# Second-half low parts of each weight tile on GpSimd instead of VectorE, in a hybrid attention encoder step

## The reference, cut to what matters

```
z = einsum('bld,dc->blc', h, w_in)          # one input projection
fq, fk, fv, fg, ff, sq, sk, sv, sg = split(z)
fo = fox_attention(fq, fk, fv, lf) * silu(fg)      # 16 heads, forget gates, causal
so = swa_attention(sq, sk, sv, sinks, rel_bias) * silu(sg)   # 16 heads, 4 kv heads, window 128
out = einsum('blc,cd->bld', concatenate([fo, so]), w_out)
y = layer_norm(ALPHA * h + out, ln_g, ln_b)
```

## Time and profile before

| | |
|---|---|
| median of 3 runs | 1078.89 us (1078.78 to 1079.07) |
| the profiled execution | 1078.65 us, span of the trace 1077.1 us |
| PE busy | 1053.2 us (98%) |
| DVE busy | 609.4 us (57%) |
| ACT busy | 436.6 us (41%) |
| POOL busy | 50.4 us (5%) |
| low halves on DVE (L796) | 132, mean 1222 ns, 160.3 us |

### The profile page before, as it was taken

The page is one execution under the profiler, slowest core; times in us unless marked ns, Lnnn a source line. Parts: engine busy times, 40 slices in busy tenths (PEclk is TensorE's granted clock), DMA queues, the critical chain, the costliest instruction groups (busy, mean ns, idle before and its releaser), DMA issues.

```text
span 1077.1 us, 20572 instructions
## 1 busy us (share of the span) xinstructions
PE 1053.2 (98%) x7617; PEld 983.4 (91%) x7617; DVE 609.4 (57%) x1493; ACT 436.6 (41%) x1078; POOL 50.4 (5%) x99
## 2 busy tenths in 40 slices
PE   7999999999999999999999999999999999999996
PEld 7999999999999999999999999999999878888885
DVE  6655465554546455364654676554776674333486
ACT  6444344443444344443444454344544553211310
POOL 1010000000000000000010000000000000000000
PEclk9999999999999999999999999999999999999998
DMA  9142223222222312313612212122122144222423
GB/s 334 54 137 90 75 98 108 92 72 100 89 71 100 108 56 85 108 63 110 200 68 92 87 46 78 52 91 96 48 78 77 56 170 163 78 78 83 185 65 117
DMA packets 20810, 106.65 MB, mean 99 GB/s; under 512 B 3216, under 2 KB 3632, under 8 KB 11488
## 3 DMA queue, kind: packets, MB, share of 16 engines
q1 hardware_dynamic: 14960, 83.13, 21.6%
q0 software_dynamic: 5808, 22.95, 6.5%
HBM read 95.18 MB, written 14.17 MB: 102 GB/s over the span
## 4 chain that ended last, share of the span: by engine, by line
PE 91%; DVE 4%; issue 3%; ACT 1%; DMA 0%; DVEq 0%; ACTq 0%; SPq 0%
PE ps L1142 58%; PE ps L1289 18%; PE ps L1259 5%; PE ps L1237 4%; PE ps L1221 2%; PE ps L1220 2%; DVE small L888 1%; DVE tb L874 1%; PE ps L1172 1%; PE ps L1273 1%; ACT wh L619 0%; DMA x_raw<-in_xT 0%; DVE tb L905 0%; DVE small L901 0%; DVE wl L796 0%
## 5 line engine op out<-in xcount | busy, mean ns | idle before, releaser
L1142 PE MATMUL ps<-xh,wh 128*128 128x288 f32 (+1 forms) x1664 | 506.6, 304 | 0.0
L1142 PE MATMUL ps<-xl,wh 128*128 128x288 f32 (+1 forms) x1664 | 493.6, 297 | 0.0
L1142 PE MATMUL ps<-xh,wl 128*128 128x288 f32 (+1 forms) x1664 | 493.2, 296 | 0.0
L1142 PEld LDWEIGHTS ps<-xh,wh 128*128 128x128 f32 x1664 | 313.9, 189 | 8.7 <-issue 7.2
L1142 PEld LDWEIGHTS ps<-xl,wh 128*128 128x128 f32 x1664 | 314.1, 189 | 0.0
L1142 PEld LDWEIGHTS ps<-xh,wl 128*128 128x128 f32 x1664 | 313.5, 188 | 0.0
L796 DVE TENSOR_TENSOR wl<-w_raw,wh 128x1024 fp32r<-128x1024 f32 x132 | 160.3, 1222 | 76.5 <-ACT wh L619 74.0
L1289 PE MATMUL ps<-wh,mix_parts 128*128 128x512 f32 x576 | 185.4, 391 | 0.0
L665 ACT ACTIVATE tb<-tb,small 128x256 f32<-128x256 f32 (+5 forms) x160 | 82.6, 516 | 214.8 <-DVE small L884 135.2
L619 ACT ACTIVATE wh<-w_raw 128x1024 fp32r<-128x1024 f32 x132 | 137.9, 1053 | 77.1 <-PE ps L1289 70.5
L1289 PEld LDWEIGHTS ps<-wh,mix_parts 128*128 128x128 f32 x576 | 108.2, 188 | 22.5 <-DVE mix_parts L1012 0.3
(11 more groups left out here) (112 smaller groups left out, 854.4 us busy)
## 6 DMA issues: line engine op xcount, KB each, us to landing
w_raw<-in_w_all SPq DMA_DIRECT2D x66, 1024.0 KB, 4.8
cbc<-c_rows POOLq DMA_DIRECT2D x16, 360.0 KB, 4.1
x_raw<-in_xT SPq DMA_DIRECT2D x7, 592.0 KB, 9.7
rows<-in_x_p POOLq DMA_DIRECT2D x4, 1024.0 KB, 5.3
out_y_p<-rows SPq DMA_DIRECT2D x16, 256.0 KB, 2.5
rel_copies<-rel_rows POOLq DMA_DIRECT2D x1, 3072.0 KB, 15.8
out_fvT<-vT POOLq DMA_DIRECT2D x8, 296.0 KB, 2.4
out_fkT<-kT POOLq DMA_DIRECT2D x8, 296.0 KB, 2.4
```

The lines of the kernel that those rows point to most:

```text
L1142: ins = nc.tensor.matmul(ps[:, st.bank(k, h), 0:width], a[k % 2][:, w], b[:, ko, first:first + width], start=(ko == 0 and i == 0), stop=(k ...
```

## The change

In every stretch but the opening and the final one, half 1 of each weight tile's low part is computed by POOL (a new `weights_low` there) and no longer by DVE. `w_low` becomes two semaphores, one per half, with every wait counted anew. POOL's program no longer runs each stretch as one short list: it now follows the steps as the others do, with its DMA issues put at the steps `scores_done`, `values_done` and `STEPS + 1`, and `weights_low` at step 5 of each tile. The `rel_copies` DMA and the wait for it stay ahead of the stretch's steps. 48 of the 132 halves move (28 in the Fox loop, 20 behind it).

```diff
@@ -475,23 +475,24 @@
                                      (sink[:], sinks.partition_broadcast(P))):
                         sp.dma_start(dst, src).then_inc(small_loaded, 16)
 
-            def load_weights(n, slot, halves):
-
-                sp.wait_ge(w_high, halves)
-                sp.wait_ge(w_low, halves)
+            def load_weights(n, slot, split):
+
+                for half in range(2):
+                    sp.wait_ge(w_low[half], split)
                 sp.dma_start(w_raw[slot][:], w_all[bass.ds(n, 1)].rearrange("a p n -> p (a n)")
                              ).then_inc(w_loaded[slot], 16)
 
 
-            load_weights(2, 0, 3)
+            load_weights(2, 0, 1)
             with sp.Fori(1, W_TILES // 2 - 1) as j:
-                load_weights(2 * j + 1, 1, 4 * j)
-                load_weights(2 * j + 2, 0, 4 * j + 2)
-            load_weights(W_TILES - 1, 1, 2 * W_TILES - 4)
+                load_weights(2 * j + 1, 1, 2 * j)
+                load_weights(2 * j + 2, 0, 2 * j + 1)
+            load_weights(W_TILES - 1, 1, W_TILES - 2)
 
             for i, (dst, src) in enumerate(((gain, ln_g), (shift, ln_b))):
                 sp.wait_ge(w_high, 2 * (W_TILES - 1 + i))
-                sp.wait_ge(w_low, 2 * (W_TILES - 1 + i))
+                for half in range(2):
+                    sp.wait_ge(w_low[half], W_TILES - 1 + i)
                 sp.dma_start(dst[:], src.partition_broadcast(P)).then_inc(norm_loaded, 16)
             for i, m in enumerate(last_order):
                 for j in range(NORM_CUTS):
@@ -550,48 +551,64 @@
                                    .broadcast_to([N_HEADS, P, REL])).then_inc(bias_copied, 16)
                     pool.wait_ge(bias_copied, 16)
                 if kv is not None:
-
-                    for h in range(2):
-                        pool.wait_ge(evacuated[h], st.n0 + 1)
                     row = (kv if st.own is Fox else kv - FOX_PAIRS) * P
-                    out = fvT if st.own is Fox else svT
-                    pool.sem_inc(pool_passed, 1)
-                    pool.dma_start(out[bass.ds(row, P), :], vT[:]).then_inc(v_stored, 16)
-                if st.own is Fox:
-                    pool.wait_ge(c_stored, 16)
-                    if before:
-                        pool.wait_ge(score_read, Fox.base(g))
-                    pool.sem_inc(pool_passed, 1)
-                    for head in range(2):
-                        pool.dma_start(cbc[:, head, :], c_rows[bass.ds(2 * g + head, 1), :]
-                                       .rearrange("a n -> (a n)").partition_broadcast(P)
-                                       ).then_inc(row_terms_loaded, 16)
-                if st.own is Swa:
-                    pool.wait_ge(score_read, Swa.base(g))
-                    pool.sem_inc(pool_passed, 1)
-                    if st.kind is Fox:
-
-                        nc.gpsimd.memset(bias[0:CHUNK, :, 3 * CHUNK:], NEG).then_inc(bias_masked, 1)
-                        pool.wait_ge(bias_masked, 1)
-                        nc.gpsimd.memset(bias[CHUNK:P, :, 0:CHUNK], NEG).then_inc(bias_masked, 1)
-                        pool.wait_ge(bias_masked, 2)
-                    load_bias(g)
+                scores_done = st.score_at[-1] + 2 if before else st.begin
+                values_done = st.value_at[-1] + 1 if before else st.begin
+                for s in range(st.begin, st.end + 1):
+                    k, r = divmod(s, STEPS)
+                    if k < len(st.tiles) and r == 5 and not st.first:
+                        weights_low(st.n0 + k + 1, (k + 1) % 2)
+                    if kv is not None and s == (st.begin if st.first else STEPS + 1):
+                        for h in range(2):
+                            pool.wait_ge(evacuated[h], st.n0 + 1)
+                        out = fvT if st.own is Fox else svT
+                        pool.sem_inc(pool_passed, 1)
+                        pool.dma_start(out[bass.ds(row, P), :], vT[:]).then_inc(v_stored, 16)
+                    if st.own is Fox and s == scores_done:
+                        pool.wait_ge(c_stored, 16)
+                        if before:
+                            pool.wait_ge(score_read, Fox.base(g))
+                        pool.sem_inc(pool_passed, 1)
+                        for head in range(2):
+                            pool.dma_start(cbc[:, head, :], c_rows[bass.ds(2 * g + head, 1), :]
+                                           .rearrange("a n -> (a n)").partition_broadcast(P)
+                                           ).then_inc(row_terms_loaded, 16)
+                    if st.own is Swa and s == scores_done:
+                        pool.wait_ge(score_read, Swa.base(g))
+                        pool.sem_inc(pool_passed, 1)
+                        if st.kind is Fox:
+
+                            nc.gpsimd.memset(bias[0:CHUNK, :, 3 * CHUNK:], NEG).then_inc(bias_masked, 1)
+                            pool.wait_ge(bias_masked, 1)
+                            nc.gpsimd.memset(bias[CHUNK:P, :, 0:CHUNK], NEG).then_inc(bias_masked, 1)
+                            pool.wait_ge(bias_masked, 2)
+                        load_bias(g)
+                    if kv is not None and s == scores_done:
+                        if before:
+                            pool.wait_ge(scored, st.kind.base(st.g) + st.kind.PIECES)
+                        pool.sem_inc(pool_passed, 1)
+                        pool.dma_start(kc[:], k_cache[bass.ds(kv, 1)].rearrange("a p n -> p (a n)")
+                                       ).then_inc(k_cached, 16)
+                    if kv is not None and s == values_done:
+                        if before:
+                            pool.wait_ge(valued, 5 * st.g + 5)
+                        pool.sem_inc(pool_passed, 1)
+                        pool.dma_start(v_nat[:, V_CACHE, :], v_cache[bass.ds(kv, 1)].rearrange("a p n -> p (a n)")
+                                       ).then_inc(v_cached, 16)
                 if kv is not None:
-                    if before:
-                        pool.wait_ge(scored, st.kind.base(st.g) + st.kind.PIECES)
-                    pool.sem_inc(pool_passed, 1)
-                    pool.dma_start(kc[:], k_cache[bass.ds(kv, 1)].rearrange("a p n -> p (a n)")
-                                   ).then_inc(k_cached, 16)
-                    if before:
-                        pool.wait_ge(valued, 5 * st.g + 5)
-                    pool.sem_inc(pool_passed, 1)
-                    pool.dma_start(v_nat[:, V_CACHE, :], v_cache[bass.ds(kv, 1)].rearrange("a p n -> p (a n)")
-                                   ).then_inc(v_cached, 16)
                     for h in range(2):
                         pool.wait_ge(evacuated[h], st.n0 + len(st.tiles))
                     out = fkT if st.own is Fox else skT
                     pool.sem_inc(pool_passed, 1)
                     pool.dma_start(out[bass.ds(row, P), :], kT[:]).then_inc(k_stored, 16)
+
+            def weights_low(n, slot):
+
+
+                pool.wait_ge(w_high, 2 * n + 2)
+                a = slice(W_LEN // 2, W_LEN)
+                nc.gpsimd.tensor_tensor(wl[slot][:, a], w_raw[slot][:, a], wh[slot][:, a].bitcast(F32),
+                                        ALU.subtract).then_inc(w_low[1], 1)
 
             whole(pool, run)
 
@@ -794,7 +811,7 @@
                 dve.wait_ge(w_high, 2 * n + half + 1)
                 a = slice(half * (W_LEN // 2), (half + 1) * (W_LEN // 2))
                 nc.vector.tensor_tensor(wl[slot][:, a], w_raw[slot % 2][:, a], wh[slot][:, a].bitcast(F32),
-                                        ALU.subtract).then_inc(w_low, 1)
+                                        ALU.subtract).then_inc(w_low[half], 1)
 
             def silu(st, k, h):
 
@@ -945,7 +962,7 @@
                         else:
                             dve.wait_ge(w_high, i - 1)
                         nc.vector.tensor_tensor(wl[slot][:, a], w_raw[slot][:, a], wh[slot][:, a].bitcast(F32),
-                                                ALU.subtract).then_inc(w_quarter_low if i < 2 else w_low, 1)
+                                                ALU.subtract).then_inc(w_quarter_low if i < 2 else w_low[i // 4], 1)
                 dve.wait_ge(small_loaded, 4 * 16)
                 bias_table()
                 dve.wait_ge(zeros, 6)
@@ -1026,7 +1043,7 @@
                         mixed_low(0)
                     if r == 0 and 1 <= k <= len(st.tiles):
                         read_out(st, k - 1, 1)
-                    if k < len(st.tiles) and r in (1, 5):
+                    if k < len(st.tiles) and (r == 1 or r == 5 and st.first):
                         weights_low(st.n0 + k + 1, (k + 1) % 2, r // 4)
                     if st.first and s == SUMS_AT:
                         gate_sums()
@@ -1131,7 +1148,7 @@
 
                     pe.wait_ge(evacuated[h], 1 if st.first and k == 2 else n)
                 if h == 0 and quarter % 2 == 0:
-                    pe.wait_ge(w_low, 2 * n + quarter // 2 + 1)
```

(7 more changed lines are left out.)

## The result

| | before | with the change |
|---|---|---|
| median | 1078.89 us (1078.78 to 1079.07, 5 runs) | 1104.83 us (1103.39 to 1104.95, 5 runs) |
| ratio | | 1.0238, 95% interval 1.0224 to 1.0252 |
| span of the trace | 1077.1 us | 1103.3 us |
| mean granted clock of PE | 0.997 | 0.992 |

What follows compares the result with a forecast made beforehand. PE was taken to bound the kernel. Holds in the short stretches (+6.5) and the 3 MB copy (+2.0) added 8.5 us to the profiled 1078.65; with 0.24 to the median, 1087.4 us, range 1077.8 to 1092.

Steps and rivals of the forecast that it cites:

- What bounds the kernel: Whole kernel: PE bounds it, and the most the change can give is 2.9 us, from six waits for the scaling.
- POOL's time: One low half of 1024 elements on POOL: 2.3 us, with bounds of 1.67 and 3.3.
- The hold: DVE beside POOL's subtraction: its next instruction reading two SBUF inputs stands still until POOL has ended.
- Where the hold costs nothing: Fox stretches: the held mask addition moves the scaling by 2.14 us, 1.0 us of cover is left, so no loss.
- The short stretches: Step 5 of six short stretches: holds delay PE by 0.93 us twice and 1.15 four times, +6.5 in place of -2.9.
- chain of 0.89 us: Short stretches: time from the start of the minimum (L890) to PE's start, without the subtraction L796.
- The 3 MB copy: Stretch after the Fox loop: POOL's first low half waits behind `rel_copies` and makes PE late, +2.0 us, once.
- No hold: Rival: POOL and DVE run side by side, the six waits vanish, only `rel_copies` is paid: 1078.0 us, chance 0.20.
- POOL is slow: Rival: the subtraction takes 3.3 us or more, or hinders DVE in the Fox loop too: 1094 us and more, chance 0.10.

Runs made afterwards that it cites:

- e6: The change with POOL's subtraction replaced by a memset of the same 128x1024, those low parts left out of the products: 1074.83 us, one run.
- e12: The change with POOL's subtraction in eight pieces, the 3 MB copy's wait moved to the bias loads, ACT's copies ahead of the newer exp: 1073.48 us.
- e4: The change with ACT's copies of the transposed rows put ahead of the newer unit's exp in each step: 1082.94 us, ratio 1.0034.
- e5: The change with POOL's subtraction of 1024 elements cut into eight of 128, back to back: 1077.53 us, ratio 0.9986.

## Why the prediction was right or wrong

**What bounds the kernel** was right: PE, with few waits, and a best case of a few microseconds. Its size was read from the wrong row: 2.9 us by PE's waits, 4.3 by those of the weight loads. The versions with no hold or a small one gained 4.1 (e6) and 5.4 us (e12, which includes the ACT wait).

**POOL's time** was right: 2.3 forecast, 2.38 measured. Half of the Trainium skill's 4497 ns, an estimate of 2.25, is nearly as close (GPSIMD Engine Reference, Performance versus the Vector engine).

**The hold** was right, in kind, victim and length: 2.26 us for the minimum (L890 before), 2.32 for the mask addition.

**"Where the hold costs nothing" is the step that failed.** It followed only unit 1: mask, maximum, exp, scaling, and found 1.0 us of cover in front of PE. That path did have cover. The hold also delays whatever DVE does next, so unit 2's exp; and behind this exp, in ACT's in-order list, stood the copies that free PE's transpose bank. There the cover was 0.1 us, to be read from rows of the trace before. Eight times 1.64 to 1.77 us make 13.4 us that the sum had at zero. e4 shows it: with ACT's two calls swapped the Fox loop has no wait while all holds stay.

**The short stretches** were forecast at +6.5 and lost 7.9. Mechanism and place were right, but that the term came so near is in part luck, since two errors worked against each other. The ACT queue, some 0.5 us per stretch, was left out. And the delay by the scaling alone was put too high: in e4, with the queue out of the way, the six steps between matched matmuls are 0.7 to 1.0 us, 5.3 together, where the forecast had 0.93 and 1.15. (By its own chain of 0.89 us behind 596.93 the smaller should have been 0.85.) The whole kernel e4 is 3.9 us above before.

**The clock** was not in the sum: 4.5 us for three dips behind pauses of about 2 us.

**The 3 MB copy** was forecast at +2.0, and cost nothing in the change. The forecast took the copy's 15.8 us over unchanged. The late half itself made the copy faster, by 2.3 to 3.3 us, since it held back the weight load that ran beside it. With PE on time and the half uncut (e4) there is no wait. That of 1.6 us in e5 has another cause, a piece held by DVE.

**The rivals.** "No hold" fell to the two DVE groups above. "POOL is slow" named the right symptom, holds that cost in the Fox loop too, but tied it to a POOL time of 3.3 us. At 2.38 us it was already so. The forecast gave this case 0.10 and cut the range at 1092.

## What to carry to other kernels

When an instruction gets later, follow not only its own result but everything that stands behind its reader in that engine's in-order list: the cover that counts is the smallest of these, and it can be 0.1 us beside a path with 1.0. An elementwise instruction moved to POOL and reading SBUF is worth cutting into pieces: those of 0.47 us caused no wait of PE in the Fox loop and 0.1 us or less in a short stretch. POOL's longer total time (3.5 us instead of 2.4 for a half) mattered at one place of 48. Idle time of PE is best read beside that of its weight loads, since the first understates what a wait costs.

## What the runs showed of the hardware that was not expected

- POOL's instruction of 470 ns in a queue of eight lets DVE in after each piece: holds of 0.1 to 0.3 us, with no sign of DVE being kept out to the queue's end. Where DVE's subtraction began first, POOL's piece stood for it, 1.44 us (e5).
- A POOL memset of 955 ns holds no two-input DVE instruction, a POOL copy of 1046 ns holds it to its end (the mask addition took up to 1.05 us).
- Of the six PE pauses in the short stretches of the profiled execution, three (1.87 to 1.99 us) were followed by 3.4 us at 1.2 GHz and three (1.71, 1.72 and 1.99 us) were not; pauses of 1.2 to 1.5 us (e4) were followed by none.
- The 3 MB copy inside HBM took 12.5 to 13.5 us in the seven traces where the next 1 MB load had to wait, and 15.3 to 15.8 us in the seven with that load beside it.
